# Row order of the last two panels, and who adds row 1, at two hand-overs of a two-block model

## The reference

```python
mix = jnp.concatenate([y_ssm, y_ml, y_fx, y_pool], axis=-1) @ w_out[l]   # 256x2048 @ 2048x2048
h = h + rmsnorm(mix, g_post_mix[l])
hn = rmsnorm(h, g_pre_ffn[l])
ff = jnp.square(jax.nn.relu(hn @ mlp_w1[l])) @ mlp_w2[l]                 # 256x8192 @ 8192x2048
h = h + rmsnorm(ff, g_post_ffn[l])
...
h = rmsnorm_2(x, attn_norm[l])                                           # second block, layer 0
proj = h @ w_in[l]
```

## Time and profile before

| | |
|---|---|
| median of 3 runs | 3332.38 us (3332.06 to 3332.95) |
| the profiled execution's own time | 3333.41 us |
| its span | 3331.6 us |
| TensorE busy | 3279.9 us, 98% |
| VectorE, ScalarE, GpSimd busy | 1928.5 (58%), 1495.9 (45%), 288.3 us (9%) |
| mean granted clock of TensorE | 0.998 |
| read from HBM | 594.86 MB, 179 GB/s over the span |

### The profile page before, as it was taken

How to read it: one execution, slowest core, us unless ns; L and a number is a source line. 1 busy time by engine, 2 the same in 40 slices (tenths; PEclk the granted TensorE clock), 3 DMA queues, 4 the chain that set the end, 5 groups by cost and what they waited for, 6 DMA issues and landing times.

```text
span 3331.6 us, 44733 instructions
## 1 busy us (share of the span) xinstructions
PE 3279.9 (98%) x17215; PEld 2808.9 (84%) x17215; DVE 1928.5 (58%) x2147; ACT 1495.9 (45%) x1693; POOL 288.3 (9%) x255
## 2 busy tenths in 40 slices
PE   6999999999999999999999999999999999999998
PEld 6998888888888788888888888888888888888887
DVE  6878565555444545565555555565556555555555
ACT  4334454344434444544344444444454434444444
POOL 5433010000000114100000000001410000000000
PEclk9999999999999999999999999999999999999999
DMA  6444655655555455455555666655545555566664
GB/s 190 143 140 129 203 179 185 191 188 189 195 193 190 161 172 177 152 170 184 189 189 183 191 193 191 195 180 172 177 152 171 195 189 189 184 191 192 191 195 144
DMA packets 234356, 598.49 MB, mean 180 GB/s; under 512 B 16136, under 2 KB 57320, under 8 KB 225016
## 3 DMA queue, kind: packets, MB, share of 16 engines
q1 hardware_dynamic: 232792, 589.06, 55.5%
q0 software_dynamic: 1312, 7.41, 0.7%
q10 hardware_dynamic: 144, 0.52, 0.0%
HBM read 594.86 MB, written 2.10 MB: 179 GB/s over the span
## 4 chain that ended last, share of the span: by engine, by line
PE 93%; DVE 3%; issue 1%; POOL 1%; DVEq 1%; ACT 1%; POOLq 0%; ACTq 0%
PE ps L624 21%; PE ps L1028 21%; PE ps L1253 19%; PE ps L630 11%; PE ps L560 10%; PE ps L978 2%; PE ps L699 1%; PE ps L700 1%; PE ps L701 1%; DVE wlo L2006 1%; PE ps L1010 1%; PE ps L1145 0%; PE ps L1144 0%; DVE wlo L2596 0%; PE ps L1179 0%
## 5 line engine op out<-in xcount | busy, mean ns | idle before, releaser
L2006 DVE TENSOR_TENSOR wlo<-raw,whi 128x2048 fp32r<-128x2048 f32 (+2 forms) x426 | 975.1, 2289 | 773.1 <-ACT whi L1368 772.7
L1368 ACT CAST whi<-raw 128x2048 fp32r<-128x2048 f32 (+2 forms) x427 | 809.5, 1896 | 753.6 <-PE ps L630 438.8
L624 PE MATMUL ps<-xT,whi 128*128 128x512 f32 x3072 | 733.0, 391 | 0.0
L624 PEld LDWEIGHTS ps<-xT,whi 128*128 128x128 f32 x3072 | 564.6, 188 | 109.4
L1028 PE MATMUL ps<-whi,stage 128*128 128x512 f32 x2048 | 489.8, 389 | 0.0
L1028 PEld LDWEIGHTS ps<-whi,stage 128*128 128x128 f32 x2048 | 384.1, 188 | 79.6
L1253 PE MATMUL ps<-whi,xT 128*128 128x512 f32 (+1 forms) x1792 | 444.4, 389 | 0.9 <-DVE wlo L2596 0.9
L630 PEld LDWEIGHTS ps<-xT,wlo 128*128 128x128 f32 x3072 | 393.9, 191 | 15.0
L630 PE MATMUL ps<-xT,wlo 128*128 128x256 f32 x3072 | 398.5, 283 | 0.0
L1253 PEld LDWEIGHTS ps<-whi,xT 128*128 128x128 f32 x1792 | 326.3, 188 | 63.6 <-issue 1.7
L2596 DVE TENSOR_TENSOR wlo<-raw,whi 128x2048 fp32r<-128x2048 f32 (+2 forms) x125 | 272.6, 2181 | 181.3 <-ACT whi L1778 181.3
(11 more groups left out here) (418 smaller groups left out, 2887.3 us busy)
## 6 DMA issues: line engine op xcount, KB each, us to landing
raw<-in_mlp_w SPq DMA_DIRECT2D x128, 1024.0 KB, 5.1
raw<-in_w_up SPq DMA_DIRECT2D x128, 1024.0 KB, 5.2
raw<-in_w_down SPq DMA_DIRECT2D x128, 1024.0 KB, 5.5
raw<-in_w_in SPq DMA_DIRECT2D x100, 1024.0 KB, 5.1
raw<-in_w_o SPq DMA_DIRECT2D x32, 1024.0 KB, 5.5
raw<-in_w_out SPq DMA_DIRECT2D x16, 1024.0 KB, 5.0
raw<-in_w_in SPq DMA_DIRECT2D x16, 832.0 KB, 4.4
raw<-in_w_uq SPq DMA_DIRECT2D x4, 1024.0 KB, 5.1
```

Of the source, the lines that this page charges most:

```text
L624: mm(psum(bank + j), whi[:, u % 2, c:c + P], xT[:, k, :], start=k == 0, stop=False)
L1368: act.copy(whi[:, u % 2, 0:width], raw[:, u, 0:width]).then_inc(sig["hi"], 1)
L2006: tt(wlo[:, u % 2, 0:width], raw[:, u, 0:width], whi[:, u % 2, 0:width].bitcast(F32), SUB).then_inc(sig["lo"], 1)
```

## The change

- In both products the last two panels are taken together: row block 0 goes through panel 14 and 15 (`mix_last_two`), or panels 2 and 3 of the last quad (`last_two`), and then row block 1 does. `pan` rises for both in the second half.
- `first_panel` moves on both engines from ahead of `post` to between the two row blocks: on ScalarE behind row 0's root, on VectorE behind row 0's four scaled chunks. `total(1)` comes behind it.
- Of row 1's four additions VectorE takes three: chunk 0 as before, and chunks 2 and 3 after all four chunks are scaled and GpSimd's is done. GpSimd takes chunk 1 alone. The step count of `mo1` falls to 1.

The diff, without blank lines:

```diff
 NORM = dict(ss=1, rsr=1, tr=8, trhi=8, xt=8)
 STAGES = dict(
     first_norm=dict(ss=1, rsr=1, xn=2, tr=KD, trhi=KD, xt=KD), w_in1=dict(quad=10, tile=18, evA=36),
-    w_out=dict(quad=5, done=3), post=dict(sq=RT, ssum=RT, ss=RT, mo0=CHUNKS, mo1=2, resid0=CHUNKS, resid=CHUNKS),
+    w_out=dict(quad=5, done=3), post=dict(sq=RT, ssum=RT, ss=RT, mo0=CHUNKS, mo1=1, resid0=CHUNKS, resid=CHUNKS),
     pre_ffn=NORM, up=dict(quad=16, tile=48, uph=64, upd=64), down1=dict(quad=16, sth=64, stl=64, done=RT * CHUNKS - 1),
     pre_attn=NORM, attn=dict(quad=16, done=31, evA=17, evD=17),
     lora_norm=dict(ss=1, rsr=1, tr=3, trhi=3, xt=3), rope=dict(rope=2),
...
                     pe.wait_ge(sig["upd"], up_at["upd"] + 57 + 4 * r + n)
-                def four(Q, k4, start, stop):
-                    for u in range(4):
+                def some(Q, k4, panels, start):
+                    for u in panels:
                         need_panel(Q, u)
                         pe.wait_ge(sig["stl"], k4 + u + 1)
                         panel_rows(u % 2, chunks, lambda part, r: stage[:, u, part * SEQ + r * P:part * SEQ + (r + 1) * P],
-                                   start and u == 0, stop and u == 3, free=left if start and u == 0 else None,
-                                   done=stop and u == 3).then_inc(sig["pan"], 1)
-                four(Q, at["stl"], True, False)
+                                   start and u == 0, False, free=left if start and u == 0 else None).then_inc(sig["pan"], 1)
+                def last_two(Q, k4):
+                    for r in range(RT):
+                        for u in (2, 3):
+                            if r == 0:
+                                need_panel(Q, u)
+                                pe.wait_ge(sig["stl"], k4 + u + 1)
+                            for n in range(4):
+                                for part, w in ((0, whi), (1, whi), (0, wlo)):
+                                    t = part * SEQ + r * P
+                                    last = mm(psum(4 * r + n), stage[:, u, t:t + P], w[:, u % 2, n * 512:n * 512 + 512],
+                                              start=False, stop=u == 3 and w is wlo)
+                                if u == 3 and (r, n) != (1, 3):
+                                    last.then_inc(sig["done"], 1)
+                            if r:
+                                last.then_inc(sig["pan"], 1)
+                some(Q, at["stl"], range(4), True)
                 with pe.Fori(1, 15) as i:
-                    four(Q + i, at["stl"] + 4 * i, False, False)
-                four(Q + 15, at["stl"] + 60, False, True)
+                    some(Q + i, at["stl"] + 4 * i, range(4), False)
+                some(Q + 15, at["stl"] + 60, range(2), False)
+                last_two(Q + 15, at["stl"] + 60)
             pe.wait_ge(sig["ld_cst"], 16)
...
                                 c = kk * 1024 + n2 * 512
                                 last = mm(psum(mix_bank(r, 2 * half + n2)), lhs, w[:, n % 2, c:c + 512],
                                           start=at_k == kk == part == 0 and w is whi,
-                                          stop=at_k == 7 and kk == part == 1)
-                        if i == 15 and (r, n2) != (1, 1):
-                            last.then_inc(sig["done"], 1)
+                                          stop=half == 0 and at_k == 7 and kk == part == 1)
                 last.then_inc(sig["pan"], 1)
             between = {3: lambda: ml_scores(1), 7: lambda: ml_scores(3), 8: lambda: ml_out(3)}
             then = {0: lambda: ml_scores(0), 2: lambda: ml_out(0), 4: lambda: ml_out(1), 5: lambda: ml_scores(2),
                     6: lambda: ml_out(2), 9: ml_in}
             pool_mix()
-            for n, (kind, i) in enumerate(MIX_PANELS):
+            def mix_last_two(first):
+                for r in range(RT):
+                    for n, i in ((first, 14), (first + 1, 15)):
+                        if r == 0:
+                            need_panel(Q, n)
+                        k0 = 2 * MIX_ORDER[i % 8]
+                        for n2 in range(2):
+                            for kk in range(2):
+                                for part, w in ((0, whi), (1, whi), (0, wlo)):
+                                    t, c = part * SEQ + r * P, kk * 1024 + n2 * 512
+                                    last = mm(psum(mix_bank(r, 2 + n2)), xT[:, k0 + kk, t:t + P], w[:, n % 2, c:c + 512],
+                                              start=False, stop=i == 15 and kk == 1 and w is wlo)
+                            if i == 15 and (r, n2) != (1, 1):
+                                last.then_inc(sig["done"], 1)
+                        if r:
+                            last.then_inc(sig["pan"], 1)
+            for n, (kind, i) in enumerate(MIX_PANELS[:-2]):
                 need_panel(Q, n)
                 if kind == "mix":
                     mix_panel(n, i, between.get(n))
...
                     glu_panel(n, i)
                 if n in then:
                     then[n]()
+            mix_last_two(len(MIX_PANELS) - 2)
             sums = st.stage("post")
             at = norm("pre_ffn", sums, sums["mo0"])
             down1(up(at))
...
                               accum_out=ss_parts[:, 4 * r + n:4 * r + n + 1])
                 return last
-            def post(at, scale, bank_of=lambda r, n: 4 * r + n, chunks=range(CHUNKS)):
+            def post(at, scale, between, bank_of=lambda r, n: 4 * r + n, chunks=range(CHUNKS)):
                 for r in range(RT):
+                    if r:
+                        between()
                     last = square_chunks(r, chunks, bank_of, scale(r), at)
                     last.then_inc(sig["sq"], 1)
...
             sums = {**at, **st.stage("post")}
             pre, _, then = norm("pre_ffn", cols[:, V_PRE_FFN:V_PRE_FFN + KD], 12288, R_FFN)
-            first_panel("up")
-            post(sums, lambda r: 1.0, mix_bank, (2, 3))
+            post(sums, lambda r: 1.0, lambda: first_panel("up"), mix_bank, (2, 3))
             def rope_sines():
...
             at = down1(up(then, {3: rope_sines}))
-            first_panel("attn", panel_width(0))
             act.wait_ge(sig["rsr"], pre["rsr"] + 1)
-            post({**at, **st.stage("post")}, lambda r: rs[:, R_FFN + r:R_FFN + r + 1])
+            sums = {**at, **st.stage("post")}
+            post(sums, lambda r: rs[:, R_FFN + r:R_FFN + r + 1], lambda: first_panel("attn", panel_width(0)))
             split(st.peek("attn")["quad"], 1, panel_width(1))
...
                     four(i)
                 return at
-            def post(gains_loaded, scale=None, bank_of=lambda r, n: 4 * r + n):
+            def post(gains_loaded, between, scale=None, bank_of=lambda r, n: 4 * r + n):
                 at = st.stage("post")
...
                 s0 = scales(0)
                 for n in range(CHUNKS):
                     normed(0, n, s0).then_inc(sig["mo0"], 1)
-                    if n == 2:
-                        total(1)
+                between()
+                total(1)
                 s1 = scales(1)
                 dve.wait_ge(sig["ld_xr"], 16)
-                for n in range(CHUNKS):
-                    last = normed(1, n, s1)
-                    if n < 2:
-                        dve.drain()
-                        dve.wait_ge(sig["resid0"], at["resid0"] + n + 1)
-                        tt(x[:, 1, chunk(n)], x[:, 1, chunk(n)], mo[:, 1, chunk(n)], ADD).then_inc(sig["resid"], 1)
-                    else:
-                        last.then_inc(sig["mo1"], 1)
+                def added(n):
+                    dve.wait_ge(sig["resid0"], at["resid0"] + n + 1)
+                    tt(x[:, 1, chunk(n)], x[:, 1, chunk(n)], mo[:, 1, chunk(n)], ADD).then_inc(sig["resid"], 1)
+                normed(1, 0, s1)
+                dve.drain()
+                added(0)
+                normed(1, 1, s1).then_inc(sig["mo1"], 1)
+                for n in (2, 3):
+                    normed(1, n, s1)
+                dve.drain()
+                dve.wait_ge(sig["resid"], at["resid"] + 2)
+                for n in (2, 3):
+                    added(n)
             dve.wait_ge(sig["ld_dt"], 16)
...
                 ts(rcos[:, :, :], rcos[:, :, :], -2.0, 1.0, MUL, ADD)
-            first_panel("up")
-            post(1, bank_of=mix_bank)
+            post(1, lambda: first_panel("up"), bank_of=mix_bank)
             then = norm("pre_ffn", cols[:, V_PRE_FFN:V_PRE_FFN + KD], R_FFN, 2, rope_angles)
             down1(up(then, {4: rope_cosines}))
             ffn_scale = lambda r: rs[:, R_FFN + r:R_FFN + r + 1]
-            first_panel("attn", panel_width(0))
-            post(2, ffn_scale)
+            post(2, lambda: first_panel("attn", panel_width(0)), ffn_scale)
             def add_half(at, first, half, bank, last_pan, scale=None, final=False):
...
                         pool.wait_ge(sig["mo0"], at["mo0"] + n + 1)
                         c = slice(n * 512, (n + 1) * 512)
```

(6 more changed lines are left out.)

## The result

The changed kernel takes 3342.35 us (median of 8, 3338.72 to 3343.02), the kernel before 3332.36 us (median of 8) beside it: a ratio of 1.0028, 95% interval 1.0019 to 1.0038. It is about 10 us slower. The prediction had the sign and the places, but 6 of the 10 us: 3338.3, with a range up to 3341.3. The profiled execution took 3343.02 us, with a span of 3341.2.

What follows compares the result with a forecast made beforehand. TensorE, busy 98% of the span, was taken to bound the kernel. +1.3 us at the first hand-over and +4.65 at the second sum to 5.95: 3332.38 + 5.95 = 3338.3 us, range 3334.3 to 3341.3.

Steps and rivals of the forecast that it cites:

- the waits for the last panel: Last two panels of both products: TensorE waits 1.86 us (output) and 2.13 us (down) for the last panel's low part.
- first hand-over: From the output product to the first up product: first up matmul at 443.75 instead of 442.49, +1.3 us.
- the split between the rows: Both hand-overs: the first panel's split, between the rows, delays row 1's total to 435.65 and 1151.65.
- the port: Both hand-overs: VectorE and GpSimd instructions with both operands in SBUF hold each other up.
- The hold: Second hand-over: GpSimd's 3.79 us low part starts about 0.15 us first; VectorE's additions wait, ending at 1160.85 and 1161.5.
- the clock: Rival: the granted clock falls to 0.5 in the second hand-over, 3339.8 to 3341.3, say 3340.2 us; chance 30%.
- a drop at the first hand-over: A fallen clock from the output product to the first up product: counted at nothing, would make the time worse.
- row 0's sums came no sooner: Last two panels of both products: row block 0's sums were forecast 1.4 and some 1.2 us sooner than before.
- Second hand-over: From the down product to layer 0's first projection: sixth projection matmul at 1164.65 instead of 1160.05, +4.65 us.

Runs made afterwards that it cites:

- e9: Changed kernel with 9 of the 12 row-1 matmuls of the panel before last moved ahead of the last panel's row-0 half: 3341.29 us, 1.0025.
- e6: Kernel before with only the first panel's split moved between the rows: 3337.40 us, 1.0014.
- e10: e9 with GpSimd's low part of the second projection panel behind VectorE's additions, and more fillers (24 instead of 12, 3 before the second transposes): 3335.43 us, 1.0008.
- e1: Changed kernel with GpSimd's low part of the second projection panel waiting for VectorE's additions of the second hand-over: 3336.30 us, 1.0012.
- e2: Changed kernel with row 1's additions shared as before (VectorE 0 and 1, GpSimd 2 and 3): 3336.33 us, 1.0011.
- e4: Kernel before with only the new sharing of row 1's additions: 3337.64 us, 1.0016.
- e5: e4 with GpSimd's low part of the second projection panel waiting for VectorE's additions: 3332.90 us, 1.0001.
- e7: Changed kernel with more filler products of TensorE in the stops of both hand-overs (19 instead of 12 at first, others before later transposes): 3339.83 us, 1.0021.
- e3: Changed kernel with the last two panels one after the other again in both products: 3340.28 us, 1.0025.
- e8: e5 with more fillers in both hand-overs (16 instead of 12, and 4 before the second pair of transposes): 3331.73 us, 0.9996.

## Why the prediction was wrong

**Right: the waits for the last panel.** 1.86 and 2.13 us forecast, 1.66 and 2.04 measured. They come from the two slots of the split panel, and in the down product from the low part of the left operand, which VectorE makes behind the panel's; nothing of the change moves those. That they are not paid again behind VectorE's split, as the working had it for the first hand-over, is what e9 shows.

**Right: the split between the rows.** Total of row 1 at the first hand-over at 435.65 - 0.7 forecast, 434.76 measured. e6 prices it at 4.8 us by itself with its fallen clock, e10 at 2.4 without one.

**Right: the port.** The hold was forecast in full, about 3.5 us later additions, with GpSimd first by 0.15 us, and measured as that (0.14 us, additions 4.70 us for 1.29, so 3.4). e1, e2, and e4 against e5 show it as the largest single cause. The Trainium skill (SBUF — State Buffer, "SBUF: two separate sides") says that the later of two such instructions is blocked for the whole of the earlier one; the run shows it for one of 3.70 us, which the profile before could not.

**Wrong: the clock.** The step that failed is in the sum of the first hand-over, which was made at full clock and "a drop at the first hand-over, which I count at nothing"; the clock stood only as a rival for the second, at 30%, from a stop near 3.9 us, and the down matmuls behind TensorE's stop were taken at full speed. In the changed kernel it fell at the first hand-over, inside the last two down panels and twice in the second:

- First hand-over: forecast +1.3, measured 24.75 - 21.70 = +3.05 up to the first up matmul. With the clock kept (e7) it is 22.80 - 21.70 = +1.1, so the working was right at full clock and 1.95 us are the clock. From there to the last two down panels it takes 0.5 us longer than before (694.80 against 694.28), since the first up matmuls were slow as well.
- Down panels: the chain shows the 24 matmuls behind the stop, with 24 x 0.2268 = 5.44 us at full clock:

```profile
1144.55 7.34 PE ps L672 x24
```

- Row 1's first scaled chunk is 1157.40 - 1139.63 = 17.77 behind the beginning of the last two panels, against 1151.57 - 1136.77 = 14.80 before: +2.97 where +1.2 was forecast. In e2, where the clock did not fall there, it is 16.48, +1.7. For the same reason row 0's sums came no sooner (total at 1149.97 - 1139.63 = 10.34, before 1147.05 - 1136.77 = 10.28), though the working had 1.2 us; in e2 it is 9.05.
- Second hand-over in all: the first projection matmul at 1168.07 - 1139.63 = 28.44 instead of 1159.10 - 1136.77 = 22.33: +6.1. The first 16 projection matmuls then took 3.91 us instead of 3.27: +0.6. That is 6.7 where 4.65 was forecast. e10, without the hold and without a fall, has +1.5 up to the sixth projection matmul; with 3.4 for the hold that is 4.9, so here too the working was right at full clock, and 1.8 us are the clock.

3.05 + 0.5 + 6.1 + 0.6, less the 0.7 us by which everything began earlier, is the 9.6 us by which the spans differ. The clock has 1.95 + 0.5 + 1.8, some 4.2 us, of it, and 4 us are what the forecast lacked. This account rests on one trace of each kernel. In the times e7 gives back 2.5 us, which its trace bears out; the 1.1 us of e9 are within the spread of the runs.

**Open.** Whether the panel order helps or hurts by itself is not settled: with the new sharing it costs about 2 us (changed against e3), with the old it gains 0.7 to 1.1 (e2 against e6), neither far outside the spread of the runs. Nor is it settled why the clock stays in one execution and falls in another with the same stops (e2 and the changed kernel in the down panels): the changed kernel's eight times spread over 4.3 us.

## What to carry to other kernels

When work is moved between two engines that share a port, look at what stands next in the queue of the engine that is relieved: it now starts sooner, and here a 3.7 us instruction started 0.14 us ahead of the two short additions on the critical path. One wait on it, which cost nothing in e5 since its result is wanted later, was worth 6 of 10 us. Add up the idle pieces of TensorE around a stage boundary before lengthening them, as here the clock was lost behind several short stops too; and to have sums complete earlier, first see which panel's split they wait for.

## What the runs showed of the hardware

The clock fell under shorter stops than the earlier trace rows had led me to expect. In the changed kernel's down product a single stop of 2.04 us between full-speed matmuls was followed by a granted clock of 0.50 from about 1.0 us after the matmuls had begun again until 1149.0. In e2 the same stop of 2.04 us was followed by a clock of 1.00. In the first hand-over of the changed kernel the clock fell at about 439.0, behind a stop of 2.03 us, 8 transposes and within a second stop of 0.92 us. e4 and e5 have the same stops before their first two pairs of transposes in the first hand-over (1.49 and 1.27 us, 1.48 and 1.26 us), and only in e4's profile did the clock fall there. So stops of this length do not decide it by themselves. With more fillers of 128 columns by the identity it was at 1.00 through both hand-overs in the profiles of e7, e8 and e10.
